# The normed token rows of a hybrid layer kernel stored last token first, and the output projection's trips written out on two engines

## What is computed

```python
xn = _rmsnorm(h, norm1_g[l])
proj = xn @ w_in[l]                 # q, k, v, forget; conv B, C, h; GLA q, k, v, r; three gates
...
mix = (jax.nn.sigmoid(g_a + gbias[:D_MODEL]) * ya
       + jax.nn.sigmoid(g_b + gbias[D_MODEL:2 * D_MODEL]) * yb
       + jax.nn.sigmoid(g_c + gbias[2 * D_MODEL:]) * yc)
h = h + mix @ w_o[l]

u = _causal_dwconv(_rmsnorm(h, norm2_g[l]) @ w_up[l], mlp_conv_w[l])
u_gate, u_up = jnp.split(u, 2, axis=-1)
h = h + (jax.nn.silu(u_gate) * u_up) @ w_down[l]
return _rmsnorm(h, final_norm_g)[:, N_META:]
```

## Time and profile before

| | |
|---|---|
| median of 3 runs | 1746.51 us (1746.36 to 1746.97) |
| the profiled execution, span from first to last instruction | 1745.1 us |
| TensorE busy | 1734.3 us, 99%, 13429 matmuls |
| VectorE busy | 1117.8 us, 64% |
| ScalarE busy | 763.7 us, 44% |
| GpSimd busy | 263.3 us, 15% |
| DMA | 320.62 MB, mean 184 GB/s |

### The profile page before, as it was taken

One profiled execution on the slowest core, in us unless ns is written; L12 is line 12 of the kernel. 1 busy time (PEld: TensorE's weight loads), 2 busy tenths in 40 slices (PEclk: granted clock), 3 DMA queues, 4 the chain that ended last, 5 costly groups with the idle time before them and its releaser, 6 DMA issues.

```text
span 1745.1 us, 34098 instructions
## 1 busy us (share of the span) xinstructions
PE 1734.3 (99%) x13429; PEld 1680.7 (96%) x13429; DVE 1117.8 (64%) x1607; ACT 763.7 (44%) x921; POOL 263.3 (15%) x494
## 2 busy tenths in 40 slices
PE   9999999999999999999999999999999999999998
PEld 8999999999999999999999999999999999888886
DVE  6857766667565554555556687777777777554454
ACT  6635444354354444444444444334444444343433
POOL 3153332630530000000000043321000000000000
PEclk9999999999999999999999999999999999999999
DMA  8567557666565655556645566666555565665654
GB/s 232 169 180 186 168 149 198 176 175 178 153 184 181 189 178 178 175 182 194 201 159 192 181 195 192 204 200 192 183 182 181 180 186 180 223 190 189 189 192 134
DMA packets 310296, 320.62 MB, mean 184 GB/s; under 512 B 17353, under 2 KB 285133, under 8 KB 310093
## 3 DMA queue, kind: packets, MB, share of 16 engines
q1 hardware_dynamic: 296861, 311.01, 58.2%
q0 software_dynamic: 12928, 7.80, 2.0%
q10 hardware_dynamic: 432, 0.79, 0.1%
HBM read 311.10 MB, written 2.11 MB: 179 GB/s over the span
## 4 chain that ended last, share of the span: by engine, by line
PE 99%; DVE 0%; DMA 0%; ACT 0%; SPq 0%; issue 0%; ACTq 0%; DVEq 0%
PE ps L1435 27%; PE ps L1437 27%; PE ps L1436 27%; PE ps L1693 5%; PE ps L1692 5%; PE ps L1691 5%; PE ps L1526 0%; DMA xb<-in_x_dram 0%; PE ps L1540 0%; PE ps L1565 0%; PE ps L1555 0%; PE ps L1556 0%; PE ps L1584 0%; PE ps L1585 0%; DVE xl L941 0%; DVE lo L896 0%
## 5 line engine op out<-in xcount | busy, mean ns | idle before, releaser
L896 DVE TENSOR_TENSOR lo<-raw,hi 128x1024 fp32r<-128x1024 f32 x584 | 709.9, 1229 | 494.4 <-ACT hi L627 490.2
L1435 PE MATMUL ps<-xh,hi 128*128 128x260 f32 (+1 forms) x3328 | 945.8, 284 | 0.2 <-DVE xl L941 0.2
L1437 PE MATMUL ps<-xh,lo 128*128 128x260 f32 (+1 forms) x3328 | 941.7, 283 | 0.0
L1436 PE MATMUL ps<-xl,hi 128*128 128x260 f32 (+1 forms) x3328 | 936.5, 281 | 0.0
L627 ACT CAST hi<-raw 128x1024 fp32r<-128x1024 f32 x584 | 604.8, 1048 | 671.8 <-PE ps L1437 539.0
L1436 PEld LDWEIGHTS ps<-xl,hi 128*128 128x128 f32 x3328 | 626.6, 188 | 0.2
L1435 PEld LDWEIGHTS ps<-xh,hi 128*128 128x128 f32 x3328 | 625.2, 188 | 1.3 <-issue 0.4
L1437 PEld LDWEIGHTS ps<-xh,lo 128*128 128x128 f32 x3328 | 624.7, 188 | 0.0
L610 POOL DMA_DIRECT2D hT<-h2b x128 | 69.6, 553 | 604.3 <-DVE h2b L1289 599.7
L1693 PE MATMUL ps<-lo,act_h 128*128 128x512 f32 x350 | 138.5, 396 | 0.0
L1692 PE MATMUL ps<-hi,act_l 128*128 128x512 f32 x350 | 137.3, 392 | 0.0
(11 more groups left out here) (298 smaller groups left out, 1383.6 us busy)
## 6 DMA issues: line engine op xcount, KB each, us to landing
raw<-in_w_in_dram SPq DMA_DIRECT2D x224, 512.0 KB, 3.6
raw<-in_w_up_dram SPq DMA_DIRECT2D x176, 512.0 KB, 4.6
raw<-in_w_down_dram SPq DMA_DIRECT2D x88, 512.0 KB, 4.7
raw<-in_w_o_dram SPq DMA_DIRECT2D x32, 512.0 KB, 3.4
raw<-in_w_in_dram SPq DMA_DIRECT2D x32, 256.0 KB, 4.2
raw<-in_w_a_o_dram SPq DMA_DIRECT2D x16, 512.0 KB, 4.3
raw<-in_w_b_o_dram SPq DMA_DIRECT2D x16, 512.0 KB, 3.3
raw<-in_w_c_o_dram SPq DMA_DIRECT2D x16, 512.0 KB, 3.3
```

The costliest lines, as they stand in the source:

```text
L896: nc.vector.tensor_tensor(part(ph, i, q, lo_all), raw[:, s, :], part(ph, i, q, hi_all).bitcast(F32), ALU.subtract).then_inc(lo_ready, 1)
L1435: nc.tensor.matmul(acc, w_hi, mh, start=first and j == 0, stop=False)
L1436: nc.tensor.matmul(acc, w_hi, ml, start=False, stop=False)
L1437: ins = nc.tensor.matmul(acc, w_lo, mh, start=False, stop=last and j == KJ - 1)
```

## The change

`xh` and `xl` keep their names, sizes and places, but are now views that run backwards over the rows that are allocated: token t of a block stands at column 271 - t. Everything that uses them goes through these views. So ACT and DVE write the rows from the high address to the low (L647, L941, L799, L1274), DVE reads `xh` in the same direction, and TensorE reads the moving operand with a step of minus one element. hT, `bo_h`, `mix_h`, `act_h` and their partners, the weights and PSUM stand as before. The window of tokens 12 to 271 is columns 259 down to 0 of a row, where it was columns 12 up to 271.

WO's loop over four trips is written out on ACT and on DVE; the loops of SP and TensorE over the same trips stay.

```diff
--- before.py
+++ after.py
@@ -196,8 +196,9 @@
         bf = sb("bf", [FH, 1])
 
         xn_scope = ExitStack()
-        xh = sb("xh", [P, KT, T], F32R, xn_scope)
-        xl = sb("xl", [P, KT, T], F32R, xn_scope)
+        xh_rows = sb("xh", [P, KT, T], F32R, xn_scope)
+        xl_rows = sb("xl", [P, KT, T], F32R, xn_scope)
+        xh, xl = xh_rows[:, :, ::-1], xl_rows[:, :, ::-1]
 
         pro = ExitStack()
         xa = sb("xa", [P, XC], F32, pro)
@@ -788,7 +789,7 @@
             with act.Fori(1, GT.trips) as i:
                 gate_trip(i, False)
 
-            with act.Fori(0, WO.trips) as i:
+            for i in range(WO.trips):
                 for q in range(WO.n):
                     round_panel(WO, i, q + LOOK)
                     if q % 4 == 3:
@@ -1256,7 +1257,7 @@
             link(nc.vector.memset(sqsum[:], 0.0))
             linked(0)
             straight_done()
-            with dve.Fori(0, WO.trips) as i:
+            for i in range(WO.trips):
                 for q in range(WO.n):
                     split_panel(WO, i, q + LOOK)
                     if q % 4 == 3:
```

## The result

The changed kernel takes 1759.52 us (median of 3 runs, 1759.42 to 1759.84) against 1746.51: a ratio of 1.0074, 95% interval 1.0058 to 1.0090. It is slower by 13.0 us. The profiled execution spans 1757.6 us, 12.5 more than before.

What follows compares the result with a forecast made beforehand. The prediction took TensorE's own stream to bound the kernel. All terms were 0, so 1745.1 + 0 = 1745.1 us of span, plus 1.4 us between span and median, gave 1746.5 us; range 1724 to 1780 us.

Steps and rivals of the forecast that it cites:

- What bounds the kernel: TensorE's own matmul stream sets the end nearly everywhere, busy 1734.3 of 1745.1 us; other engines count only where TensorE waits.
- Part 1: TensorE's 9984 matmuls on xh and xl read the moving operand backwards: taken as 0, bounded above by +1153 us.
- rival C: On TensorE, weight load and backward moving read cross: +3 ns on 9984 matmuls, +30 us, 1776 us; chance 0.14.
- Rival D: TensorE fetches each backward word alone: +1153 us, about 2900 us; chance 0.18.
- Rival E: TensorE's matmuls get a better alignment: -2 ns on 9984, -20 us, 1726.5 us; chance 0.10.
- Parts 2 and 3: ACT and DVE working backwards, in the prologue and at the end of WO's half trips: each taken as 0.
- Rival B: Only DVE and ACT pay, in the prologue: +1.6 to +3.1 us, at worst twice that; chance 0.08.
- Part 4: WO's loop written out on ACT and DVE removes register instructions while TensorE is busy throughout: taken as 0.

Runs made afterwards that it cites:

- the benchmarks: Separate kernels without the layer, output zeros: groups of 120 or 150 equal fp32r matmuls back to back, varying place, width, step and direction; 260 columns upwards averaged 119.7 ns.

## Why the prediction was right or wrong

**What bounds the kernel: right.** TensorE's stream sets the end; the loss is in it, and nothing upstream took part.

**Part 1, TensorE reads backwards: this is the step that failed.** I put it at 0, between the ends -2 and +3 ns a matmul and the +1153 us of unpaired words. It is about +1.6 ns on 8640 matmuls, 14.0 us, and about -0.9 ns on the 1344 of 272 columns, 1.2 us less. The rows had shown equal matmuls of one line with durations 5 ns apart, which I put down to where their operands lie, and a stream over its clock. They suggested that a new layout may give a new pitch, and that hitting the old one to 0.35 ns, which "within 0.2%" needed, was not the likeliest case. I gave it 0.55.

The argument for 0 was that the new window is the mirror image of the old. But it also begins at another place of the 64 bytes, and neither the place nor the direction is neutral. From before to the kernel over the same words backwards is +1.1 ns, and from there to the changed kernel +0.6; by the other way round, +1.1 for the place and +0.6 for the direction. The two don't simply add, and a share for each can't be given. Why they cost what they cost stays open. The range held the time only because it took in rival C's 30 us.

The pitches I worked from were low, since a stretch counts what is under way. By starts they are 118.9 ns for 260 columns, 125.3 for 272 (I had 123.5) and 231.2 for 512. Twelve columns from 260 to 272 then cost 6.4 ns and the 240 after them 105.9, so there is no one price for a column.

**Rival C was the case that came.** It had the sign, the stages (UP and GT with a new pitch, mix_h and bo_h with their old) and the size of one matmul within a factor of two, 3 ns for 1.6; its time, +30 us, is over twice the 13.0. Its picture, the weight load upwards and the tokens downwards and the two crossing, was not shown: no trace tells in which direction the weight load reads, and weights a quarter as wide did not free the moving read.

**Rival D: the price right, the condition not met.** I put an unpaired matmul of 260 columns at 118.6 + 114.8 = 233.4 ns; the step of 2 words took 233.3. That it agrees to 0.1 ns is luck, as both terms are a little off. By what the Trainium skill states of one 16-byte line ("SBUF — State Buffer", Door 1) a step of 2 would be free, since two of its words share a line, and yet the pitch doubled; for this operand the measurement decides. By what the Trainium skill states of VectorE's ports ("Vector Engine (DVE) Microarchitecture Reference", section 5.2), it is runs of adjacent words that keep the full rate. TensorE's rows follow that, in falling order too.

**Rival E, a better alignment, did not occur.** No arrangement of the layer ran faster than the kernel before.

**Parts 2 and 3, backwards on ACT and DVE: right, 0.** Kernel after, against the earlier trace rows:

```profile
L648 ACT ACTIVATE xh<-hT,g 128x272 fp32r<-128x272 f32 x16 | 7.5, 515 | 1.1 <-DVE hT L935 0.7 <-DVE hT L948 0.3
L942 DVE SCALAR_TENSOR_TENSOR xl<-hT,g,xh 128x272 fp32r<-128x272 f32 x16 | 7.5, 504 | 0.4 <-ACT xh L648 0.4
...
L800 ACT ACTIVATE xh<-hT,par 128x258 fp32r<-128x258 f32 x16 | 7.2, 497 | 0.0
...
L1275 DVE SCALAR_TENSOR_TENSOR xl<-hT,par,xh 128x258 fp32r<-128x258 f32 x16 | 7.1, 485 | 0.3
```

515, 504, 497 and 485 ns where they were 515, 509, 496 and 485 (the xl instructions in the prologue read and write backwards, and are no slower). Rival B did not occur.

**Part 4, the trips written out: right, 0**, measured by itself.

## What to carry to other kernels

In a kernel whose matmuls run back to back, the layout of an operand is a cost of the same order as the small edits one makes: moving one by 16, 32 or 48 bytes changed this kernel by 4 to 10 us out of 1747, and it can be had or lost without touching an instruction. After any change of layout or direction read the pitch of a long stretch, count over time, for each stage apart. When an operand must be read backwards, this case has 0.6 to 1.4 ns on matmuls of 260 columns, about 1%, not a doubling; at 256 and 272 columns it went either way. When a small benchmark is to speak for a kernel, compare equal addresses, with where the tensor itself begins counted in. When a forecast of "no change" rests on thousands of equal instructions, divide the bound of "no change" by their number first: here it left 0.35 ns for each.

## What the runs showed of the hardware

- In the benchmarks fp32r matmuls with 128x128 weights cost 111.7 ns at 192 columns in either direction and at 128 downwards, 118.3 to 120.0 at 256, 173.3 at 384 and 226.7 to 230.0 at 512, at a granted clock of 1.00. From 320 to 512 columns at word 12 it is 0.434 ns a column upwards and 0.451 downwards. The limit per column that I took from the slope in the earlier trace rows is so only in part.
- There is no such value for 128 columns upwards. That group came first in its kernel; its 120 matmuls and 27 of the next group took about 213 ns each, up to 41.7 us. The trace's first record of a granted 2.4 GHz begins at that moment; for the time before it there is none, although the rows print 1.00.
- A moving operand with a step of 2 words costs double, steps of 3 and 4 about the same as 2.
- Downwards the pitch of 260 columns held 120.0 ns over nearly all places of row and weights and for weights of 32 to 128 columns; upwards it lay between 116.7 and 121.7.
- The benchmarks show nearly the layer's dependence on place with TensorE alone at work (DMA share 0.00 to 0.01), so other engines are not needed for it.
- Not settled: why 118.8 rather than 119.9 ns comes with one place and not with the next, why one and the same group (260 columns, word 20, downwards) had 122.2 ns in one benchmark and 120.0 in another, and in which direction weights are read.
